# A mixture-of-experts stage on one core: the steps of unequal pieces are replaced by steps of one expert and of two halves

## The reference, cut to what matters

```
xb = x_pad[tok]                                   # the rows of the tokens that chose expert e
hid = jax.nn.silu(xb @ w_gate[e]) * (xb @ w_up[e])
y.at[tok].add((hid @ w_down[e]) * wt[:, None])
```

## Time and profile before

| | us |
|---|---|
| median of 3 runs | 1819.23 |
| the profiled execution, its own time | 1841.76 |
| its span, first to last instruction | 1839.9 |
| stage of the routed experts (first gate-up product to the end of the last down product) | 830.2 to 1720.5 |
| TensorE busy in the span | 1726.3 (94%) |
| weights moved in the stage | 61 x 3 loads of 1024 KB |
| rows gathered and scattered (DMA queue q0) | 34.09 MB |

### The profile page before, as it was taken

The page is one execution under the profiler, slowest core; times in us unless marked ns, Lnnn a source line. Parts: engine busy times, 40 slices in busy tenths (PEclk is TensorE's granted clock), DMA queues, the critical chain, the costliest instruction groups (busy, mean ns, idle before and its releaser), DMA issues. The chain is left out here.

```text
span 1839.9 us, 18149 instructions
## 1 busy us (share of the span) xinstructions
PE 1726.3 (94%) x6713; PEld 809.0 (44%) x6714; DVE 471.8 (26%) x1149; ACT 270.1 (15%) x670; POOL 270.1 (15%) x199
## 2 busy tenths in 40 slices
PE   5999999999998889969999999999999999999687
PEld 4777696666665679635422222222222222221233
DVE  5223222222233472562111111111011010000176
ACT  2111202222222530101100100101000000000110
POOL 5333411010112131001100000100000000000000
PEclk9999995555555999979999999999999999999898
DMA  7224220001101022609968768777866655560380
GB/s 218 58 60 125 55 81 14 21 11 27 30 23 45 23 76 69 251 12 393 346 237 321 271 260 312 284 279 294 316 260 241 239 203 204 220 234 31 126 357 35
DMA packets 117057, 306.38 MB, mean 167 GB/s; under 512 B 20576, under 2 KB 79104, under 8 KB 91264
## 3 DMA queue, kind: packets, MB, share of 16 engines
q1 hardware_dynamic: 104752, 271.40, 40.4%
q0 software_dynamic: 12240, 34.09, 4.7%
HBM read 289.73 MB, written 26.21 MB: 172 GB/s over the span
## 5 line engine op out<-in xcount | busy, mean ns | idle before, releaser
L1384 PE MATMUL bank<-sb_gate_up,sb_xgT 128*32 128x512 f32 (+2 forms) x1696 | 547.1, 607 | 0.8 <-DVE sb_xgT L1494 0.8
L1384 PEld LDWEIGHTS bank<-sb_gate_up,sb_xgT 128*32 128x32 f32 (+2 forms) x1696 | 111.1, 124 | 404.5 <-issue 399.0
L1408 PE MATMUL bank<-sb_down,sb_work 128*32 128x512 f32 (+2 forms) x848 | 275.7, 607 | 0.6 <-ACT sb_work L1539 0.6
L1441 POOL DMA_INDIRECT expert_rows<-sb_rows_out,sb_work x42 | 42.8, 1018 | 788.5 <-DVE sb_rows_out L1500 769.6
L393 PE MATMUL bank<-sb_x_hl,sb_w_hl 128*128 128x512 f32 x384 | 153.9, 534 | 0.0
L1508 DVE TENSOR_TENSOR sb_work<-sb_work,bank 128x256 f32<-128x256 f32 x42 | 17.8, 423 | 525.2 <-ACT sb_work L1533 525.2
L203 POOL TENSOR_TENSOR sb_w_hl<-sb_r,sb_w_hl 128x1024 fp32r<-128x1024 f32 x54 | 130.5, 2420 | 87.1 <-ACT sb_w_hl L1141 76.4
L1408 PEld LDWEIGHTS bank<-sb_down,sb_work 128*32 128x32 f32 (+2 forms) x848 | 54.9, 124 | 186.6 <-issue 184.3
L210 PE MATMUL bank<-sb_x_hl,sb_w_hl 128*128 128x512 f32 x480 | 115.0, 400 | 1.4 <-DVE sb_small L526 1.0
L364 PE MATMUL bank<-sb_work 64*128 64x128 f32 (+3 forms) x192 | 110.7, 673 | 3.1 <-DVE sb_work L542 3.1
L383 PEld LDWEIGHTS bank<-sb_work 128*128 128x128 f32 x480 | 92.7, 261 | 41.3 <-issue 22.6
(11 more groups left out here) (253 smaller groups left out, 1417.0 us busy)
## 6 DMA issues: line engine op xcount, KB each, us to landing
sb_gate_up<-in_w_gate SPq DMA_DIRECT2D x64, 1024.0 KB, 8.4
sb_gate_up<-in_w_up SPq DMA_DIRECT2D x64, 1024.0 KB, 12.0
sb_down<-in_w_down SPq DMA_DIRECT2D x64, 1024.0 KB, 5.4
sb_r<-in_w_in SPq DMA_DIRECT2D x34, 512.0 KB, 3.9
sb_rows_even<-expert_rows SPq DMA_DIRECT2D x4, 2048.0 KB, 15.8
sb_rows_odd<-expert_rows SPq DMA_DIRECT2D x4, 2048.0 KB, 19.2
sb_r<-in_w_out SPq DMA_DIRECT2D x8, 512.0 KB, 3.9
sb_w_ple_gate<-in_w_ple_gate SPq DMA_DIRECT2D x1, 4096.0 KB, 21.5
```

The source lines that it names most:

```text
L1384: last = nc.tensor.matmul(bank[BH][rows, :], xgT[:, k, rows], gate_up[slot_of[r]][:, :, k, :], start=k == 0, stop=k == KD - 1)
L1408: last = nc.tensor.matmul(bank[BO[i]][rows, :], hT[:, c, rows], Wd[slot_of[r]][:, c, i * 512:(i + 1) * 512], start=c == 0, stop=c == 1)
L1441: nc.gpsimd.indirect_dma_start(out=rows_d, out_offset=bass.IndirectOffsetOnAxis(ap=dst[:, s:s + 1], axis=0), in_=osb[s % 2], in_offset=Non ...
```

## The change: what it does, and the diff

Ranks 0 to 33 now have a capacity of 128 rows and ranks 34 to 63 one of 64. The trios are gone. There are 49 steps: 34 alone and 15 pairs. Four steps alone come first, then fifteen times a pair and two alone. The first 8 lists and gathers keep their place, LEAD and the six slots stay.

```
-NFULL = 6
-NTRIO = 14
-NPAIR = 8
+NFULL = 34
+NPAIR = 15
...
-        ("cap_col", np.where(np.arange(P) % NE < NFULL, 128, np.where(np.arange(P) % NE < NFULL + 2 * NTRIO, 96, 64))[:, None]),
+        ("cap_col", np.where(np.arange(P) % NE < NFULL, 128, 64)[:, None]),
...
-        trio = lambda a_, b_, c_: [[(a_, 0, 64, 0), (a_, 64, 32, 64), (c_, 96, 32, 0)], [(b_, 0, 64, 0), (b_, 64, 32, 64), (c_, 96, 32, 32)]]
         pair_of = lambda a_, b_: [(a_, 0, 64, 0), (b_, 64, 64, 0)]
-        steps = [full(r) for r in range(NFULL)]
-        next_small = NFULL + 2 * NTRIO
-        for g in range(NTRIO):
-            if g < NPAIR:
-                steps.append(pair_of(next_small, next_small + 1))
-                next_small += 2
-            steps += trio(NFULL + 2 * g, NFULL + 2 * g + 1, next_small)
-            next_small += 1
-        assert next_small == NE
+        steps = [full(r) for r in range(NFULL - 2 * NPAIR)]
+        for g in range(NPAIR):
+            steps += [pair_of(NFULL + 2 * g, NFULL + 2 * g + 1)]
+            steps += [full(r) for r in range(NFULL - 2 * (NPAIR - g), NFULL - 2 * (NPAIR - g) + 2)]
+        assert sorted({v[0] for u in steps for v in u}) == list(range(NE))
...
-        rank2, rank3 = wk(NOV), wk(NOV)
+        rank2 = wk(NOV)
...
-                nc.vector.tensor_scalar(q128, rank2, float(NFULL + 2 * NTRIO), 32.0, ALU.is_lt, ALU.mult)
-                nc.vector.tensor_scalar(rank3, rank2, float(NFULL), 32.0, ALU.is_lt, ALU.mult)
-                dve.drain()
-                nc.vector.tensor_tensor(q128, q128, rank3, ALU.add)
+                nc.vector.tensor_scalar(q128, rank2, float(NFULL), 64.0, ALU.is_lt, ALU.mult)
```

## The result

The changed kernel took 1541.26 us, the median of 4 runs (1523.74 to 1548.99), against 1823.62 us for the kernel before in the same comparison (4 runs, 1816.10 to 1841.64). The ratio is 0.837 (95% interval 0.825 to 0.849). The profiled execution took 1534.57 us, its span is 1532.7 us.

The account below looks back on a forecast made before the run. TensorE was taken to bound the routed experts' stage: 49 steps of about 12 us instead of 42, many of 25, make it 302 us shorter, 1819.2 - 302 = 1517 us; range 1506 to 1560.

Parts of the forecast that it names:

- The trio's steps: Routed experts' stage: pieces of 64, 32 and 32 columns don't run side by side; 25.35 us a step, 28 of 42 steps.
- Rival E: Trio's steps are no longer than others, 15.95 us being waiting time; seven more steps give 1903 us; 1%.
- The step lengths: TensorE in the routed experts' stage: 12.25 us a pair, 12.04 and 11.77 a step alone; stage 302 us shorter.
- What TensorE is fed with: Weight and row loads: 225 MB in 574 us need 392 GB/s; at 413 the last weights land 29 us ahead.
- Rival B: Weights come late and DMA becomes the bound; at 359 GB/s they land 52.5 us late, giving 1570 us; 27%.
- Notice and gathers: Loads issued 36 us before their step cover a single burst; gathers have 16 us, slowest landing found 12.9.
- rival C: Gathers take 18 us under full DMA load, each step waits 2 us, some 90 in all: 1607 us; 6%.
- Rival D: Small TensorE waits at every step lower the granted clock; at the 1.2 GHz level 2105 us, slower; 2%.
- The sum: Whole run: 302 us off the profiled 1841.8 gives 1539.8, off the median 1819.2 gives 1517 us.

Follow-up runs that it names:

- experiments 1 and 2: Experiment 1, and a second edit of the kernel before, with the 64-column piece's gate-up chunks all ahead of the 32-column ones: gate-up 14.07 us, stage 836.3 us.
- Experiment 3: Half way between both kernels, six of the fourteen trios kept (22 steps alone, 12 pairs, 12 trio's steps): stage 712.0 us.
- Experiment 4: The changed kernel loading only the first quarter of each up weight from the seventh expert on: stage 12.8 us shorter, run 1532.17 us.
- experiment 1: The kernel before, still 42 steps, with each trio's 64-row piece written as two of 32: stage 573.7 us, run 0.827 of the kernel before.
- the second look: The changed kernel run again, unedited, beside kernels of 32-column pieces: stage 594.4 us, run 1545.36 us.
- experiment 6: The changed kernel with five weight slots instead of six: stage 7.4 us longer.
- experiment 7: The kernel of experiment 1 loading only the first quarter of each up weight from the seventh expert on: stage 515.1 us.
- experiment 5: The changed kernel with all 34 steps alone first, then the 15 pairs: stage 47.9 us longer, run 1583.37 us.

## Why the prediction was right, point by point

**The trio's steps (right).** That pieces of 64, 32 and 32 columns don't run side by side was read from the timeline and shown by experiments 1 and 2. Experiment 3 shows that the price per step is additive. The prediction set the trace against a rule of the Trainium skill and gave only half of it: the page "TensorEngine Tiling (Array Packing)" says in Tiling Modes, Key Properties that different tiles can run in parallel, and in the same list that changing the tiling mode drains TensorE. The runs agree with both: two tiles of 64 or four of 32 run in parallel (7.09 and 7.07 us), and where the width changes one pass ends before the next begins (15.95 us by turns, 14.07 with a single change). Rival E, by which the trio's steps would be no longer than others, is out.

**The step lengths (mechanism right, size 8 us too high).** Predicted from one start to the next: 12.25 for a pair, 12.04 and 11.77 for the steps alone behind it, 36.06 together. Measured: 11.86, 11.89 and 11.69, 35.44. Over 15 repeats that is 9.3 us. The pair's step is 0.39 us shorter than I took it: it had been timed between a step alone and a trio's, and the list that it makes is that of a step alone (4 matmuls), not a pair's. The lists cost 0.10 us for 4 matmuls and 0.15 for 8, not the 0.14 and 0.27 taken in proportion, and the 12.04 left as it was still held the 0.41 us of 12. Experiment 4, where nothing waits, has the stage at 579.9 us; the predicted 588.4 (830.2 to 1418.6) is 8.5 above.

**What TensorE is fed with (the direction of the reading right, the margin wrong).** 392 GB/s over the stage were called enough, with 29 us in hand at 413. Measured are 384 GB/s over 592.7 us, queues at 0.95, and 12.6 us of waits and their aftermath, confirmed as DMA's by experiment 4 (12.8 us). The flaw is the 413 GB/s, which one stretch of 36 us had shown, taken as a rate for the whole stage: the queues gave 399 in the first four repeats, 411 from 1000 to 1100 us, 401 from 1100 to 1200 and 385 from 1200 to 1300. The 406 GB/s that the predicted repeat asks for are more than most of these. That the steps turned out faster made it worse: the three of a repeat asked for 14.63 MB in 35.44 us, 413 GB/s. Rival B was thus part of the outcome, at 12.6 of its 52.5 us; the worry that 359 GB/s was all that the queues could hold was not borne out, since they gave 397 over 573.7 us in experiment 1. The two errors, 8.5 too much and 12.6 too little, nearly cancel, which is luck: the stage is 592.7 (594.4 in the second look) for a predicted 588.4.

The figure of about 358 GB/s per core in the Trainium skill, "DMA: Bandwidth & Descriptors", Specifications, does not hold the kernel back here: 397 GB/s over a whole stage are above it.

**Notice and gathers.** The landing of a gather had a median of 11.2 us at full load (10.9 predicted from the earlier trace rows), and no gather was waited for; rival C is out. The notice of 36 us is nearly used up by landings of 31 us in the median; experiment 6 puts a slot's worth at 7 us.

**The clock.** Rival D did not come, but its seed did: after a wait the grant fell for the next products, 1.7 us each time in the changed kernel. The stage's clock is 0.99.

**The sum.** Against the profiled execution the prediction was 1539.8 us and the measurement is 1534.57. That it is this close is partly luck: a stage 4.3 us longer than predicted and a tail 1.3 us longer are outweighed by a stage that began 10.9 us earlier, and that goes with the attention part's clock and not with the change. The five traces with a clock of 0.55 from 280 to 600 us begin their stage at 827.1 to 833.0, the three with 0.58 or 0.59 (the changed kernel is one) at 817.8 to 822.0, whatever the kernel. Against the medians the prediction was 1517 and the measurement is 1541.26. The 22.5 us between the profiled execution of before and the median of its first runs were carried over as if they belonged to the kernel. Most likely they are the attention part's clock too, though only profiled executions show it by part. That is the largest error of the number, and it is in no step of the change.

## What to carry to other kernels

Give the pieces that share the array one width: cut a 64-column piece into two of 32 rather than put it beside 32s, even if the instructions grow by a third (48 to 64 here). When a stage on TensorE is made shorter, divide its bytes by the new length first: here 12.8 of the 310 us that TensorE gained (890.3 to 579.9) were lost to late weights, and of the next 64.8 us on TensorE (579.9 to 515.1, experiment 7) only 19.0 reached the stage (592.7 to 573.7, experiment 1). A repeating order should ask for the same bytes in each repeat: the same steps with the pairs last cost 48 us.

## What the runs showed of the hardware that was not expected

- A short wait of TensorE can cost about as much again. After 2.17 us idle the next gate-up products took 8.78 us instead of 7.09; after 5.46 us 8.77, after 4.11 us 9.93. But not always: in experiment 5 one wait of 2.34 us was followed by products of 7.09:

```profile
1342.13 9.93 PE L1373 MATMUL bank<-sb_gate_up,sb_xgT 128*64 128x512 f32 x32 [4.11 <-DMA sb_gate_up<-in_w_up]
1359.52 7.09 PE L1373 MATMUL bank<-sb_gate_up,sb_xgT 128*64 128x512 f32 x32 [2.34 <-DMA sb_gate_up<-in_w_up]
```

- The attention part, which no kernel here changes, had a mean granted clock of 0.55 from 280 to 600 us in the kernel before and of 0.68 in experiment 6, where the stage began 45 us earlier (785.1 instead of 830.2):

```profile
280.00:600.00 320.00, 307.94 (x895) 199.29 (x894) 90.64 (x356) 73.29 (x249) 42.81 (x26) 0.55 0.09 25
```

The changed kernel and experiment 6:

```profile
280.00:600.00 320.00, 307.69 (x943) 199.28 (x943) 95.45 (x378) 77.64 (x267) 44.56 (x27) 0.58 0.10 26
```

```profile
280.00:600.00 320.00, 300.12 (x1070) 199.36 (x1070) 110.89 (x414) 94.47 (x299) 46.84 (x27) 0.68 0.10 27
```

The eleven traces fall into three groups: 0.55 with a stage that begins at 827.1 to 833.0 us, 0.58 or 0.59 with 817.8 to 822.0, and 0.68 to 0.70 with 780.3 to 785.1. Each group holds different kernels, and the changed kernel stands in two of them. What decides between them is open.
